# Tiles that TensorE reads, laid at different offsets modulo 512 bytes

## The chip, the core and the metric

The kernel runs on one core of a Trainium2 chip. The metric is the device time of one execution in microseconds (us); the time before is the median of 3 runs, 2656.01 us (2654.61 to 2657.22). The profile is one profiled execution of the same program. Its engines are called PE (TensorE's matmuls), PEld (TensorE's weight loads), DVE (VectorE), ACT (ScalarE), POOL (GpSimd) and SP (SyncE, which here only issues DMAs).

## The reference, cut to what matters

Two transformer blocks over 1024 tokens of width 1024, in float32:

```python
def first_block(x, p, ...):
    h = rms_norm(x, norm_mix)
    u_pool, q, k, v, g_a, g_b = jnp.split(h @ w_in, split_at, axis=-1)
    y_a = pool_mixer(u_pool, w_pool, pool_scale)
    y_b = stick_breaking_attention(q, k, v)            # 8 heads of 64
    merged = sigmoid(g_a) * (y_a @ w_branch_a) + sigmoid(g_b) * (y_b @ w_branch_b)
    x = x + merged @ w_out
    h = rms_norm(x, norm_ffn)
    x = x + (silu(h @ w_ffn_gate) * (h @ w_ffn_up)) @ w_ffn_down   # 1024 -> 2816 -> 1024
    gate = sigmoid(rms_norm(x, norm_ple) @ w_ple_gate)
    return rms_norm(x + gate * (p @ w_ple_proj), norm_final)

def second_block(x, c, ...):
    sh1, sc1, g1, sh2, sc2, g2 = split(silu(c) @ w_ada + b_ada, 6)
    h = rms_norm(x, pre_mix_g) * (1 + sc1) + sh1
    y = token_mixer(h, ...)      # chunked mLSTM beside sliding-window attention
    x = x + g1 * rms_norm(y, post_mix_g)
    h = rms_norm(x, pre_ffn_g) * (1 + sc2) + sh2
    y = conv_ffn(h, w_up, ffn_conv_w, ffn_conv_b, w_down)          # again 2816 wide
    return x + g2 * rms_norm(y, post_ffn_g)
```

## The kernel before, in words

The activations lie transposed: 128 partitions hold channels, and the free axis holds the 1024 tokens. One matmul multiplies a 128x128 block of weights (the stationary operand, loaded by its own weight load) with 512 tokens of a 128-channel tile (the moving operand) into one bank of PSUM.

Every product is made in three matmuls. A float32 operand is split into a rounded high part (type fp32r) and the rest, the low part: ACT casts `w_raw` to `w_hi` (L1853, L1618), POOL subtracts to make `w_lo` (L3991, L3897), and likewise there are `h_hi` and `h_lo` for the activations. TensorE then adds high weights by high activations, high weights by low activations, and low weights by high activations. This order stands in every loop: in `project` (L769), `halved` (L815), `qkv_steps` (L866 to L869), `beside_steps` (L1263 to L1268), `product` (L1064) and `strassen_down` (L1094). Almost all of TensorE's work has this shape.

The two feed-forward networks use a seven-product scheme. In the up and gate projections, `product(i, j)` multiplies with one of seven combinations of halves of the activations; some of these are plain halves of `h_hi` and `h_lo`, and three are kept in tiles of their own, `form_hi` and `form_lo` in block one and `back_form_hi` and `back_form_lo` in block two. In the down projection, `strassen_down` walks 77 units (7 products of 11 row tiles each). Unit u reads `x_hi` and `x_lo` of a ring of four slots (`x_hi_a`, `x_lo_a` in block one, `x_hi_b`, `x_lo_b` in block two), which ACT (L1930) and DVE (L3069) fill from `keep_x`, or from the ring `x_ring`, which SP loads from memory (L4350). These are called combination tiles and down tiles here.

Each engine runs its own list of instructions in the order of the program, and waits on semaphores that another engine or a DMA raises. No wait depends on where a tile lies.

The tiles in on-chip memory are laid out by a stack: a tile begins where the one before it on the stack ended, rounded up to 32 bytes, and a scope that is closed gives its room back, so that tiles of different stages lie over each other. The first tile, `consts`, begins at byte 16512 of each partition. `w_raw`, `w_hi` and `w_lo` are two buffers of 1024 floats each (8192 bytes a partition), and a weight block is 128 floats, which is 512 bytes a partition. A 512-token row is 2048 bytes. From `w_raw` on, the hot tiles all have sizes that are multiples of 512 bytes, so that one offset modulo 512 holds for every block and every row of a tile. The first lines of the layout are these:

```python
consts = sb("consts", [P, N_CONST])
vecs = sb("vecs", [P, N_VEC])
ident_bf = sb("ident_bf", [P, P], BF16)
causal_bf = sb("causal_bf", [P, P], BF16)
```

with `ident_bf` and `causal_bf` of 256 bytes each ahead of `mod`, `gain`, `final_gain`, `eps_col`, `w_raw`, `w_hi`, `w_lo`, `tmp`, `norm_row`, `h_hi` and `h_lo`. `consts` begins at 128 modulo 512, `ident_bf` at 288, `causal_bf` at 32, and `w_raw` at 20224, which is 256 modulo 512; so does every later tile named so far. The tiles of the second mixer (`prob`, `o_tok`, `q_carried`, `late_consts`, `rope_mem` and others) follow small tiles and begin elsewhere.

Of the kernel before, what the change touches and what calls it, by code (L numbers as in the profile page):

```python
# [9 lines left out]
BF16 = mybir.dt.bfloat16  # L10
# [4 lines left out]
P = 128  # L15
# [4 lines left out]
HALF = 512  # L20
# [190 lines left out]
KH = KD // 2  # L211
# [137 lines left out]
def two_blocks(nc, io, known=None):  # L349
    with ExitStack() as ctx:  # L350
# [9 lines left out]
        def sb_in(scope, name, shape, dt=F32):  # L360
            return scope.enter_context(nc.sbuf_tensor(name, shape, dt))

        def sb(name, shape, dt=F32):
            return sb_in(ctx, name, shape, dt)
# [1 line left out]

        consts = sb("consts", [P, N_CONST])
        vecs = sb("vecs", [P, N_VEC])
        ident_bf = sb("ident_bf", [P, P], BF16)
        causal_bf = sb("causal_bf", [P, P], BF16)  # L370
        mod = sb("mod", [P, 6 * KD])
        gain = sb("gain", [P, 4 * KD])
        final_gain = sb("final_gain", [P, 4, KD])
        eps_col = sb("eps_col", [P, 2])
        w_raw = sb("w_raw", [P, 2, 1024])
        w_hi = sb("w_hi", [P, 2, 1024], F32R)
        w_lo = sb("w_lo", [P, 2, 1024], F32R)
        tmp = sb("tmp_mem", [P, 2, T])
        norm_row = sb("norm_row", [P, T])
        h_hi = sb("h_hi", [P, KD, T], F32R)  # L380
# [46 lines left out]
        ff1 = ExitStack()  # L427
        with ExitStack() as downs:
            keep_x_a = sb_in(downs, "keep_x_a", [P, KB, HALF])
        form_hi_mem = sb_in(ff1, "form_hi", [P, 3, KH, HALF], F32R)  # L430
        with ExitStack() as downs:
            x_ring_a = sb_in(downs, "x_ring_a", [P, 4, HALF])
            x_hi_a = sb_in(downs, "x_hi_a", [P, 4, HALF], F32R)
            x_lo_a = sb_in(downs, "x_lo_a", [P, 4, HALF], F32R)
        form_lo_mem = sb_in(ff1, "form_lo", [P, 3, KH, HALF], F32R)
        with ExitStack() as forms:
            form_raw = sb_in(forms, "form_raw", [P, 8, HALF])
# [92 lines left out]
        ys = ExitStack()  # L530
# [7 lines left out]
            keep_x_b = sb_in(downs, "keep_x_b", [P, KB, HALF])  # L538
        BACK_FORMS = (SUM_2, DIFF_3, GATE_HIGH)
        with ExitStack() as raws:  # L540
            sb_in(raws, "before_back_raw", [P, 3, KH, HALF])
            back_raw = sb_in(raws, "back_raw", [P, 3, KH, HALF])
        back_hi_mem = sb_in(ys, "back_form_hi", [P, 3, KH, HALF], F32R)
        back_lo_mem = sb_in(ys, "back_form_lo", [P, 3, KH, HALF], F32R)
        x_hi_b = sb_in(ys, "x_hi_b", [P, 4, HALF], F32R)
        x_lo_b = sb_in(ys, "x_lo_b", [P, 4, HALF], F32R)
        back_sums = sb_in(ys, "back_w_sums", [P, 2, HALF])
# [4143 lines left out]
def build(nc, arrays, known=None):  # L4691
    io = {}
    for name, v in arrays.items():
        io[name] = nc.dram_tensor(f"in_{name}", v.shape, F32, kind="ExternalInput").ap()
    for name, shape in SCRATCH.items():
        io[name] = nc.dram_tensor(name, shape, F32, kind="Internal").ap()
    io["out"] = nc.dram_tensor("out_dram", (KD, P, T), F32, kind="ExternalOutput").ap()
    return two_blocks(nc, io, known)
# [12 lines left out]
```

## Time and profile before

| | |
|---|---|
| time before, median of 3 runs | 2656.01 us |
| span of the profiled execution, first to last instruction | 2657.1 us |
| PE busy | 2566.2 us, 97% of the span, 11826 matmuls |
| PEld busy | 2080.6 us, 78% |
| DVE, ACT, POOL busy | 1776.9, 1186.2, 1173.3 us |
| mean granted TensorE clock | 0.992 of full speed |
| DMA | 311.96 MB, mean 117 GB/s |

The profiled execution has no time of its own beside its span; the span lies 1.1 us above the median and inside the spread of the three runs. The busy time of a matmul in the profile is longer than the distance to the next one (a matmul of 512 columns lasts 0.39 us, and the next begins 0.23 us after it), because matmuls are pipelined and their ends are modelled. What a matmul takes of the engine is therefore read from the distance between starts. Offsets in memory do not stand in the profile; they follow from the layout.

### The profile page before, as it was taken

The page shows a single profiled execution, that of the slowest core. Times are in us where ns is not written, and L with a number is a line of the kernel's source. Part 1 is how long each engine was busy: PE and PEld are TensorE (multiplying, and loading weights), DVE is VectorE, ACT ScalarE, POOL GpSimd, SP SyncE. Part 2 cuts the span into 40 slices and gives each one's busy share as a digit, 9 for nine tenths or more (in the row PEclk, how much of TensorE's full clock was granted, in tenths as well). Part 3 has the DMA queues.
Part 4 walks back from the last instruction along what each step waited for, and adds up shares of the span by engine and source line. Part 5 has one row for each costly group of instructions (what it writes and reads, how often), then busy time and mean ns, then how long its engine had stood idle before and what let it go on. Part 6 is the DMA issues. An engine that isn't in the chain of part 4 may idle for free.

```text
span 2657.1 us, 32148 instructions
## 1 busy us (share of the span) xinstructions
PE 2566.2 (97%) x11826; PEld 2080.6 (78%) x11826; DVE 1776.9 (67%) x2180; ACT 1186.2 (45%) x2084; POOL 1173.3 (44%) x767
## 2 busy tenths in 40 slices
PE   7999999999899999999999999999999999999997
PEld 6887788888688888888877778778767888887885
DVE  6888876653877777778854546527459666666685
ACT  6777521112533333344554333455444444444444
POOL 2444522224455555555544221124442655555456
PEclk9999999999999999999999999999999999999998
DMA  3000044433155555675622111223321222225674
GB/s 125 25 25 25 20 136 158 155 122 112 48 191 197 190 199 188 219 236 184 202 79 83 65 33 40 45 58 75 135 95 48 83 84 81 86 81 182 214 234 138
DMA packets 125916, 311.96 MB, mean 117 GB/s; under 512 B 13368, under 2 KB 26936, under 8 KB 122816
## 3 DMA queue, kind: packets, MB, share of 16 engines
q1 hardware_dynamic: 125760, 309.91, 35.5%
q8 instruction: 94, 1.54, 0.3%
q14 instruction: 62, 0.51, 0.1%
HBM read 248.45 MB, written 61.41 MB: 117 GB/s over the span
## 4 chain that ended last, share of the span: by engine, by line
PE 79%; DVE 11%; ACT 3%; issue 3%; DMA 2%; POOL 2%; SPq 0%; ACTq 0%; DVEq 0%; POOLq 0%
PE psum_mem L1064 28%; PE psum_mem L769 20%; PE psum_mem L1094 11%; PE psum_mem L1263 2%; PE psum_mem L1268 2%; PE psum_mem L1265 2%; PE psum_mem L831 2%; DMA x_ring_a<-hidden 1%; PE psum_mem L815 1%; PE psum_mem L866 1%; PE psum_mem L867 1%; PE psum_mem L869 1%; PE psum_mem L1340 1%; DVE left L2769 1%; DVE tmp_mem L3696 1%
## 5 line engine op out<-in xcount | busy, mean ns | idle before, releaser
L3991 POOL TENSOR_TENSOR w_lo<-w_raw,w_hi 128x512 fp32r<-128x512 f32 x364 | 529.1, 1456 | 550.7 <-ACT w_hi L1853 531.6
L3897 POOL TENSOR_TENSOR w_lo<-w_raw,w_hi 128x1024 fp32r<-128x1024 f32 (+2 forms) x105 | 237.0, 2257 | 618.4 <-ACT w_hi L1618 531.2
L1853 ACT CAST w_hi<-w_raw 128x512 fp32r<-128x512 f32 x364 | 225.5, 620 | 387.8 <-PE psum_mem L1094 167.3
L1064 PE MATMUL psum_mem<-h_hi,w_hi 128*128 128x512 f32 x672 | 263.9, 393 | 6.6 <-ACT norm_row L2485 3.2
L1064 PE MATMUL psum_mem<-h_lo,w_hi 128*128 128x512 f32 x672 | 262.9, 391 | 1.3 <-DVE h_lo L2970 1.3
L1064 PE MATMUL psum_mem<-h_hi,w_lo 128*128 128x512 f32 x672 | 262.5, 391 | 0.0
L769 PE MATMUL psum_mem<-h_hi,w_hi 128*128 128x512 f32 x736 | 232.0, 397 | 11.6 <-ACT h_hi L1652 9.1
L769 PE MATMUL psum_mem<-h_lo,w_hi 128*128 128x512 f32 x736 | 228.5, 392 | 5.7 <-DVE h_lo L3606 5.5
L769 PE MATMUL psum_mem<-h_hi,w_lo 128*128 128x512 f32 x736 | 227.9, 391 | 2.7 <-POOL w_lo L3897 2.7
L1618 ACT CAST w_hi<-w_raw 128x1024 fp32r<-128x1024 f32 (+2 forms) x105 | 100.2, 954 | 267.9 <-PE psum_mem L769 255.3
L769 PEld LDWEIGHTS psum_mem<-h_hi,w_hi 128*128 128x128 f32 x736 | 137.9, 189 | 43.5 <-ACT h_hi L1652 9.1
L769 PEld LDWEIGHTS psum_mem<-h_lo,w_hi 128*128 128x128 f32 x736 | 138.4, 189 | 36.7 <-DVE h_lo L3606 6.9
L769 PEld LDWEIGHTS psum_mem<-h_hi,w_lo 128*128 128x128 f32 x736 | 138.6, 189 | 32.7 <-POOL w_lo L3897 3.6
L1064 PEld LDWEIGHTS psum_mem<-h_hi,w_hi 128*128 128x128 f32 x672 | 126.8, 189 | 35.3 <-ACT norm_row L2485 4.1
L1064 PEld LDWEIGHTS psum_mem<-h_lo,w_hi 128*128 128x128 f32 x672 | 127.0, 189 | 28.4 <-DVE h_lo L2970 2.4
L1064 PEld LDWEIGHTS psum_mem<-h_hi,w_lo 128*128 128x128 f32 x672 | 126.9, 189 | 26.6
L3949 POOL TENSOR_TENSOR beta<-beta,left 128x128 f32<-128x128 f32 (+2 forms) x96 | 89.4, 932 | 123.4 <-DVE left L2769 118.3
L1263 PE MATMUL psum_mem<-h_hi,w_hi 128*128 128x512 f32 x272 | 112.8, 415 | 1.1 <-DVE tmp_mem L3309 1.1
L1268 PE MATMUL psum_mem<-h_hi,w_lo 128*128 128x512 f32 x272 | 107.2, 394 | 0.0
L1265 PE MATMUL psum_mem<-h_lo,w_hi 128*128 128x512 f32 x272 | 106.6, 392 | 0.0
L1064 PE MATMUL psum_mem<-form_lo,w_hi 128*128 128x512 f32 x264 | 103.0, 390 | 1.7 <-DVE form_lo L2968 1.7
L1064 PE MATMUL psum_mem<-form_hi,w_hi 128*128 128x512 f32 x264 | 103.0, 390 | 1.4 <-ACT form_hi L1868 1.4
(465 smaller groups left out, 6330.8 us busy)
## 6 DMA issues: line engine op xcount, KB each, us to landing
hidden<-tmp_mem SPq DMA_DIRECT2D x44, 512.0 KB, 3.5
down_sums<-sum_raw SPq DMA_DIRECT2D x22, 1024.0 KB, 5.7
w_raw<-down_sums SPq DMA_DIRECT2D x88, 256.0 KB, 4.0
w_raw<-in_w_up_b SPq DMA_DIRECT2D x44, 512.0 KB, 3.7
x_ring_a<-hidden SPq DMA_DIRECT2D x66, 256.0 KB, 4.1
x_ring_b<-hidden SPq DMA_DIRECT2D x66, 256.0 KB, 4.2
w_raw<-in_w_in_a SPq DMA_DIRECT2D x32, 512.0 KB, 3.7
ada_raw<-in_w_ada SPq DMA_DIRECT2D x64, 256.0 KB, 3.3
```

Of the source, the lines that this page charges most:

```text
L769: made = e.matmul(pairs.half(use, half), wt, x[:, half_of(half)], start=at == 0 and part == 0, stop=at == len(rhs) - 1 and part == 2, skip ...
L831: return e.transpose(out, in_, ident)
L1064: made = e.matmul(out, wt, x, start=j <= DIFF_3 and k == 0 and part == 0, stop=k == KH - 1 and part == 2, skip_group_check=True)
L1094: return e.matmul(down_bank(p, mi), w_slot(w_lo if part == 2 else w_hi, slot, of)[:, block_of(mi)], (x_lo if part == 1 else x_hi)[:, u % 4 ...
L1263: e.matmul(bank(6 + half), high, h_hi[:, k, cols], start=k == 0, stop=False, skip_group_check=True)
L1265: e.matmul(bank(6 + half), high, h_lo[:, k, cols], start=False, stop=False, skip_group_check=True)
L1268: made = e.matmul(bank(6 + half), low, h_hi[:, k, cols], start=False, stop=k == KD - 1, skip_group_check=True)
L1618: e.copy(w_hi[:, i, 0:width], w_raw[:, i, 0:width]).then_inc(*S.of("w_hi", c))
L1853: e.copy(w_slot(w_hi, slot, of), source).then_inc(*S.of("w_hi", key))
L3897: e.tensor_tensor(w_lo[:, i, 0:width], w_raw[:, i, 0:width], w_hi[:, i, 0:width].bitcast(F32), ALU.subtract).then_inc(*S.of("w_lo", c))
L3949: e.tensor_tensor(kept, kept, left[i % 3][:, HALF + 1 - width:HALF + 1], ALU.mult).then_inc(*S.of("weight", i))
L3991: e.tensor_tensor(w_slot(w_lo, slot, of), source, w_slot(w_hi, slot, of).bitcast(F32), ALU.subtract).then_inc(*S.of("w_lo", key))
```

## The change

Two things are changed, both in the layout alone. The instructions, their operands' shapes, their order and their waits stay.

First, `ident_bf` moves from before `mod` to between `w_hi` and `w_lo`, and `causal_bf` from there to behind `w_lo`. Each is 256 bytes long. So `w_raw` and `w_hi` move down by 512 bytes, `w_lo` by 256, and everything from `tmp` on stays where it was.

Second, unused pads of 32 to 128 bytes go in ahead of combination tiles and down tiles. The pads push what is behind them on the same stack: in block one also `sum_raw`, `w_sums` and `parts` (by 160 bytes) and the ring `x_ring_a` (by 32), in block two also `back_raw` (by 192), `back_w_sums` and `gate_conv_in` (by 224).

| tile | offset modulo 512 before | after |
|---|---|---|
| `w_hi`, `h_hi`, `h_lo` and the other high and low activations | 256 | 256 |
| `w_lo` | 256 | 0 |
| `form_hi`, `form_lo` | 256, 256 | 288, 416 |
| `x_hi_a`, `x_lo_a` | 256, 256 | 320, 384 |
| `back_form_hi`, `back_form_lo` | 256, 256 | 352, 448 |
| `x_hi_b`, `x_lo_b` | 256, 256 | 480, 480 |

```diff
-        ident_bf = sb("ident_bf", [P, P], BF16)
-        causal_bf = sb("causal_bf", [P, P], BF16)
         mod = sb("mod", [P, 6 * KD])
...
         w_hi = sb("w_hi", [P, 2, 1024], F32R)
+        ident_bf = sb("ident_bf", [P, P], BF16)
         w_lo = sb("w_lo", [P, 2, 1024], F32R)
+        causal_bf = sb("causal_bf", [P, P], BF16)
...
+        sb_in(ff1, "before_form_hi", [P, 8])
         form_hi_mem = sb_in(ff1, "form_hi", [P, 3, KH, HALF], F32R)
         with ExitStack() as downs:
             x_ring_a = sb_in(downs, "x_ring_a", [P, 4, HALF])
+            sb_in(downs, "before_x_hi_a", [P, 8])
             x_hi_a = sb_in(downs, "x_hi_a", [P, 4, HALF], F32R)
+            sb_in(downs, "before_x_lo_a", [P, 16])
             x_lo_a = sb_in(downs, "x_lo_a", [P, 4, HALF], F32R)
+        sb_in(ff1, "before_form_lo", [P, 32])
         form_lo_mem = sb_in(ff1, "form_lo", [P, 3, KH, HALF], F32R)
...
-            sb_in(raws, "before_back_raw", [P, 3, KH, HALF])
+            sb_in(raws, "before_back_raw", [P, 3 * KH * HALF + 48])
             back_raw = sb_in(raws, "back_raw", [P, 3, KH, HALF])
+        sb_in(ys, "before_back_form_hi", [P, 24])
         back_hi_mem = sb_in(ys, "back_form_hi", [P, 3, KH, HALF], F32R)
+        sb_in(ys, "before_back_form_lo", [P, 24])
         back_lo_mem = sb_in(ys, "back_form_lo", [P, 3, KH, HALF], F32R)
+        sb_in(ys, "before_x_hi_b", [P, 8])
         x_hi_b = sb_in(ys, "x_hi_b", [P, 4, HALF], F32R)
         x_lo_b = sb_in(ys, "x_lo_b", [P, 4, HALF], F32R)
```

## Rows read from the trace of the kernel before

**Rows 1.** The page: busy time by engine, and the granted clock in 40 slices.
```profile
PE 2566.2 (97%) x11826; PEld 2080.6 (78%) x11826; DVE 1776.9 (67%) x2180; ACT 1186.2 (45%) x2084; POOL 1173.3 (44%) x767
...
PEclk9999999999999999999999999999999999999998
```

**Rows 2.** The chain of waits, merged, longest pieces: start us, us, engine, line, count.
```profile
593.98 87.22 PE psum_mem L769 x384
...
739.78 386.58 PE psum_mem L1064 x1704
...
2063.85 353.93 PE psum_mem L1064 x1560
...
2433.44 187.07 PE psum_mem L1094 x824
```

**Rows 3.** Timeline of 1000.0 to 1000.75, PE and PEld: start us, length us.
```profile
999.94 0.39 PE L1064 MATMUL psum_mem<-form_lo,w_hi 128*128 128x512 f32 x1
999.94 0.19 PEld L1064 LDWEIGHTS psum_mem<-form_hi,w_lo 128*128 128x128 f32 x1
1000.16 0.39 PE L1064 MATMUL psum_mem<-form_hi,w_lo 128*128 128x512 f32 x1
1000.17 0.19 PEld L1064 LDWEIGHTS psum_mem<-form_hi,w_hi 128*128 128x128 f32 x1
1000.39 0.39 PE L1064 MATMUL psum_mem<-form_hi,w_hi 128*128 128x512 f32 x1
```

**Rows 4.** Groups of PE matmuls, shapes apart: line, out<-in, count, busy us, mean ns.
```profile
L1064 PE MATMUL psum_mem<-h_hi,w_lo 128*128 128x512 f32 x672 | 262.5, 391 | 0.0
...
L1064 PE MATMUL psum_mem<-form_hi,w_lo 128*128 128x512 f32 x264 | 103.2, 391 | 0.8 <-POOL w_lo L3991 0.7
...
L1064 PE MATMUL psum_mem<-back_form_hi,w_lo 128*128 128x512 f32 x240 | 93.5, 390 | 0.6 <-POOL w_lo L3991 0.6
...
L1094 PE MATMUL psum_mem<-x_hi_b,w_lo 128*128 128x512 f32 x308 | 86.2, 389 | 0.0
```

**Rows 5.** Timeline of PE at four places: bf16 matmuls of 128 and of 256 columns.
```profile
1550.88 0.23 PE L1308 MATMUL psum_mem<-band_bf,ident_bf 128*128 128x128 bf16 x1
...
1550.95 0.22 PE L1308 MATMUL psum_mem<-band_bf,ident_bf 128*128 128x128 bf16 x1
...
1572.76 0.28 PE L1308 MATMUL psum_mem<-band_bf,ident_bf 128*128 128x256 bf16 x1
...
1572.88 0.27 PE L1308 MATMUL psum_mem<-band_bf,ident_bf 128*128 128x256 bf16 x1
```

**Rows 6.** Timeline of PE at three places where a float32 weight load follows.
```profile
60.51 0.39 PE L869 MATMUL psum_mem<-h_hi,w_lo 128*128 128x512 f32 x1
60.74 0.38 PE L831 MATMUL psum_mem<-consts,beta 128*128 128x128 f32 x2
...
1567.78 0.39 PE L1268 MATMUL psum_mem<-h_hi,w_lo 128*128 128x512 f32 x1
1568.01 0.38 PE L831 MATMUL psum_mem<-consts,prob 128*128 128x128 f32 x2
...
1799.59 0.39 PE L1268 MATMUL psum_mem<-h_hi,w_lo 128*128 128x512 f32 x1
1799.82 0.38 PE L1444 MATMUL psum_mem<-state,q_carried 128*128 128x129 f32 x2
```

**Rows 7.** Groups of POOL instructions on 512 elements a partition, shapes apart.
```profile
L3897 POOL TENSOR_TENSOR w_lo<-w_raw,w_hi 128x512 fp32r<-128x512 f32 x16 | 20.8, 1300 | 134.9 <-PE psum_mem L1004 82.0 <-ACT w_hi L1618 52.9
...
L4123 POOL TENSOR_TENSOR q_carried<-q_carried,qk_ml 128x512 f32<-128x512 f32 x8 | 10.1, 1267 | 5.8 <-DMA q_carried<-w_rows 5.8
```

**Rows 8.** The page's DMA issues: engine, operation, count, KB each, us to landing.
```profile
w_raw<-in_w_up_b SPq DMA_DIRECT2D x44, 512.0 KB, 3.7
x_ring_a<-hidden SPq DMA_DIRECT2D x66, 256.0 KB, 4.1
...
rope_mem<-in_rope SPq DMA_DIRECT2D x1, 1024.0 KB, 5.6
```

**Rows 9.** The chain of waits from 1125 to 1340: the first and last DMA on it.
```profile
1178.59 3.77 DMA x_ring_a<-hidden
...
1216.11 4.23 DMA x_ring_a<-hidden
```

## Prediction

> **What bounds the kernel now.** I read the page first: PE is busy 97% of the span, the next engine, DVE, 67%, and TensorE had its full clock (2.4 GHz) in all but the last slice [rows 1]. So the time can only move much if the distance between matmuls moves. The chain of waits gives that distance without the profile's rounding, as the length of an unbroken piece by its count: 87.22 / 384 = 0.2271 us in `project`, 386.58 / 1704 = 0.2269 and 353.93 / 1560 = 0.2269 in the two up projections, 187.07 / 824 = 0.2270 in the second down projection [rows 2]. One number, 0.227 us, holds in four stages, with different tiles, weight blocks and neighbours at work. The timeline shows what lies inside it: each matmul begins with the load of the next weights beside it, 0.19 us long, and the next matmul follows at 0.22 or 0.23 [rows 3].
>
> How much of 0.227 is not streaming? Two bf16 matmuls of 128 columns start 0.07 us apart, two of 256 columns 0.12 [rows 5]: 128 more columns cost 0.05 us, one column a cycle at 2.4 GHz (0.0533). So 512 columns stream in 0.2133 us, and 0.2269 - 0.2133 = 0.0136 us of each 0.227 is something else. If that is the weight load and the stream meeting in the same place of the memory, because both tiles begin at 256 modulo 512, the change removes some of it; if it is the price of changing weights, the change does nothing. This is the question to decide.
>
> **The change part by part.** It adds and removes no instruction, wait or DMA, so nothing is queued differently, and every term is a number of matmuls by a change in their distance.
>
> What meets is the stream of one matmul and the load of the next one's weights. In the order high-high, high-low, low-high the load of `w_lo` runs beside a stream of a low tile (in `project`, with two halves, also beside its own high tile), and the load of `w_hi` beside a high or low tile. Where the activations are not moved, only the loads of `w_lo` change their distance, from 0 to 256 bytes. The groups that read `w_lo` beside unmoved activations are 672 in `product` [rows 4], and 736, 272, 144, 144, 32 for `h_hi` in the other five loops and 168 for `ya_hi`, `yb_hi`, `p_hi` and `pl_hi`, counted in the code: 2168. Where the activations are moved, all three matmuls change: 3 x (264 + 240 + 2 x 308) = 3360 [rows 4], to distances from 32 to 480. Together 5528 of some 10,000 such matmuls; the other loads of `w_hi` beside `h_hi` and `h_lo` keep distance 0.
>
> The price of a changed distance is not in this trace for the pair itself, since before all of these pairs lie at distance 0. From both sides: at best the whole 0.0136 goes, 5528 x 0.0136 = 75 us; and at worst a distance that is now clean begins to collide, by at most what the rows of float32 loads allow [rows 6]: a stream of `h_hi` (at 256) with a float32 load beside it is followed at 0.23 us, which rounding lets be 0.235, 0.008 above 0.227, 5528 x 0.008 = 44 us.
>
> Between these ends I take 0. Three readings lead there. First, one view holds distance itself apart [rows 6]: after `h_hi` comes a load of `beta` (256, distance 0), of `prob` (416, distance 160) and of `q_carried` (192, distance 448), and all three follow at 0.23 us. If distance 0 cost 0.0136, the other two should stand near 0.21 or 0.22. They carry a float32 matmul behind them instead of another fp32r, but so does the first. Second, bf16 has the same extra [rows 5]: 0.07 - 0.0533 and 0.12 - 0.1067 are both about 0.01, with the load at 288 and the stream at 160 and 416 modulo 512, and with half the bytes on both sides. A collision should depend on place or on bytes; this depends on neither. Third, the load sweeps 512 bytes within 0.19 us while the stream sweeps 2048 in 0.213 [rows 3]: they run at different speeds, so a start apart by some bytes shifts a meeting and does not avoid it.
>
> The Trainium skill says the same of the ports: in "TensorE: Matmul & The Clock Gate", section "Step-by-step: what each phase is for", TensorE has two independent read ports into the on-chip memory, so that loading the next weights takes no read bandwidth from the running matmul. By that rule this change does nothing, whatever the offsets; no run here shows the ports, and the float32 loads agree as far as 0.01 us can show [rows 6].
>
> The other engines and the DMAs touch the moved tiles too. POOL makes `w_lo`, with all three operands at 256, in 1300 ns, and `q_carried`, at 192 with others, in 1267 [rows 7]: 33 ns between them, and POOL is busy 44% [rows 1], so its slack hides either. DMAs into `x_ring_a` now land at 288 modulo 512, which is 32 past a multiple of 64. A DMA to such a place stands in the trace: `rope_mem`, at 416, 1024 KB in 5.6 us, where 512 KB to a place at 256 take 3.7 [rows 8], less than double. If the landing were longer by 0.3 us (the nearest rows lie within that), it would show only where these DMAs are on the chain, 8 times from 1178.59 to 1216.11 [rows 9]: 2.4 us. I take 0.
>
> The sum is 0 against the span of 2657.1 us. The median of the runs is 1.1 us below that span, so the forecast is the median: 2656 us.
>
> **The rivals.** *Equal offsets do collide.* For it: 0.0136 us in every matmul is unexplained, and the layout has every hot tile at one offset, so no stage of the feed-forward networks can contradict it. Against it: the bf16 pairs and the float32 loads [rows 5, 6]. If all changed pairs gain, 75 us less about 2 us, because the ring's DMAs and not the matmuls are on the chain for some 40 us (40 / 0.227 x 0.0136 = 2.4) [rows 9]: 2656 - 73 = 2583 us. If only the distance of 256 frees, 2168 x 0.0136 = 29 us: 2627. The Trainium skill has a rule that points this way: in the same page, section "Back-to-back issue gap", 512 columns cost about 216 ns at full clock. By that rule 0.011 us of 0.227 could be had, an estimate of 5528 x 0.011 = 61 us; but the chain shows 0.227 at full clock [rows 2], and the page itself ties its number to matmuls measured alone.
>
> *Unequal offsets collide.* This is the slower one: distance 0 may be the clean state, in which load and stream keep out of each other's way, and any other distance costs something. Place: the same 5528 pairs, most of them in the two feed-forward networks. Price: the float32 loads read as printed [rows 6], 0.23 - 0.227 = 0.003 us, give 17 us, 2673 us; 0.008 gives 2700. It decides from 0.001 us a pair, which is 5.5 us. Against it: the `beta` row at distance 0 also stands at 0.23, so the 0.003 belongs to the float32 neighbour.
>
> That the change doesn't reach the places it names can hardly be: the offsets follow from sizes.
>
> **How the numbers follow.** No effect 0.76, with 2651 to 2661 us, the 0.2% (5.3 us) about 2656 below which a measurement of this kernel cannot tell a change from none. Equal offsets collide 0.14, in whole or in part. Unequal offsets collide, or start-of-row penalties of the same sign, 0.10. The range takes in the first case and the small prices on either side, up to 0.002 us a pair (5528 x 0.002 = 11 us): 2645 to 2668 us, and leaves out the full gain and the larger losses, some 2 in 10. So faster by over 0.2% has 0.14, within 0.2% 0.76, slower 0.10.
>
> **What would show it.** In the profile of the changed kernel the same four pieces of the chain should again come to 0.227 us a matmul. `product` is a test in itself: its matmuls with `form_hi` and `form_lo` lie at distances of 32 and 416, and those with `h_hi` and `w_hi` beside them at 0; if the first stand at 0.213 or 0.216 and the second at 0.227, equal offsets collide, and I am wrong by the first rival. If the moved ones stand above 0.228, the second rival holds. If all stand at 0.227 and the time still moves by more than 5 us, the cause is outside TensorE, and the landing of `x_ring_a` and the mean of POOL's `w_lo` are the rows to look at.

## The result: slower, and the profile after

The changed kernel takes 2675.97 us (median of four runs, 2674.84 to 2678.59) against 2656.61 for the kernel before on the same chip: a ratio of 1.0073, with a 95% interval from 1.006 to 1.0086, or about 19 us more. The profiled execution has a span of 2674.5 us, 17.4 more than before.

The page of the changed kernel, busy time by engine and the granted clock, answers to [rows 1]:

```profile
PE 2587.3 (97%) x11826; PEld 2083.7 (78%) x11826; DVE 1780.4 (67%) x2180; ACT 1187.0 (44%) x2084; POOL 1170.2 (44%) x767
...
PEclk9999999999999999999999999999999999999999
```

PE is busy 21.1 us longer with the same 11826 instructions; ACT, DVE and POOL stay within 4 us, and the granted clock stands at 9 tenths or more in every slice. So the matmuls themselves take longer. The long pieces of its chain of waits answer to [rows 2]; the change adds seven lines of code ahead of them, so L769, L1064 and L1094 are now L776, L1071 and L1101:

```profile
595.50 87.22 PE psum_mem L776 x384
...
741.18 392.44 PE psum_mem L1071 x1704
...
2072.52 344.08 PE psum_mem L1071 x1500
...
2439.92 199.67 PE psum_mem L1101 x848
```

The first piece, in `project`, is the same to the hundredth: 87.22 us for 384 matmuls, though every load of `w_lo` in it now lies 256 bytes off. The second needs 392.44 / 1704 = 0.2303 us a matmul instead of 0.2269, the third 344.08 / 1500 = 0.2294 instead of 0.2269, the fourth 199.67 / 848 = 0.2355 instead of 0.2270. The stages whose activations were moved lost; the one where only `w_lo` moved did not.

Inside a piece, the timeline of PE (start us, length us) shows which tile it is. The first product, at 1002, and the second down projection, at 2500:

```profile
1002.11 0.40 PE L1071 MATMUL psum_mem<-form_hi,w_lo 128*128 128x512 f32 x1
...
1004.21 0.40 PE L1071 MATMUL psum_mem<-form_hi,w_lo 128*128 128x512 f32 x1
...
2501.30 1.10 PE L1101 MATMUL psum_mem<-x_hi_b,w_lo 128*128 128x512 f32 x4
...
2504.10 1.10 PE L1101 MATMUL psum_mem<-x_hi_b,w_lo 128*128 128x512 f32 x4
```

Between the first two rows lie nine starts in 2.10 us, 0.233 each; between the last two twelve in 2.80, 0.233 each.

Since the two traces hold the same 11826 matmuls in the same order, each distance can be set against its own before. Where both are below 0.3 us (no wait), the matmuls on `form_hi` and `form_lo` take 5.1 us more in all, those on `back_form_hi` and `back_form_lo` 3.3, on `x_hi_a` and `x_lo_a` 3.5, on `x_hi_b` and `x_lo_b` 6.05: 18.0 us for 3323 of the 3360 moved pairs, 0.0054 us each. The other 7933 such distances gave 3.4 us more, 0.0004 each, and the longer ones, with waits in them, 3.8 us less.

About half of these 3.4 us stand right behind the moved tiles. When `product` goes from `form` or `back_form` tiles back to `h_hi` and `h_lo`, the next nine matmuls still take 28 ns more in all than before (a mean over some 60 such places), though their own distances are 0 or 256; from the tenth on nothing is left. One such place, nine and again nine starts apart:

```profile
871.21 0.39 PE L1071 MATMUL psum_mem<-h_hi,w_hi 128*128 128x512 f32 x1
...
873.29 0.39 PE L1071 MATMUL psum_mem<-h_hi,w_hi 128*128 128x512 f32 x1
...
875.33 0.39 PE L1071 MATMUL psum_mem<-h_hi,w_hi 128*128 128x512 f32 x1
```

The first nine take 2.08 us, 0.231 each, the second nine 2.04, 0.227 each. So a pair's own distance is not the whole of it: what the pairs before it did counts too, for 1.7 us in all.

### The profile page after: what moved, and what is told of

It is laid out like the page before. It is cut to its first block, busy times and chain, and to the rows that moved or that the text cites. A ratio compares the mean times of both kernels' runs of the same rounds, so it can differ in the third digit from the quotient of the medians.

```text
span 2674.5 us, 32148 instructions
## 1 busy us (share of the span) xinstructions
PE 2587.3 (97%) x11826; PEld 2083.7 (78%) x11826; DVE 1780.4 (67%) x2180; ACT 1187.0 (44%) x2084; POOL 1170.2 (44%) x767
## 4 chain that ended last, share of the span: by engine, by line
PE 79%; DVE 11%; ACT 4%; issue 3%; DMA 2%; POOL 2%; SPq 0%; ACTq 0%; DVEq 0%; POOLq 0%
PE psum_mem L1071 28%; PE psum_mem L776 20%; PE psum_mem L1101 13%; PE psum_mem L1270 2%; PE psum_mem L1275 2%; PE psum_mem L1272 2%; PE psum_mem L838 2%; PE psum_mem L822 1%; PE psum_mem L873 1%; PE psum_mem L1347 1%; DVE left L2776 1%; PE psum_mem L876 1%; PE psum_mem L874 1%; DMA x_ring_a<-hidden 1%; PE psum_mem L1312 1%
## 5 line engine op out<-in xcount | busy, mean ns | idle before, releaser
L1071 PE MATMUL psum_mem<-h_hi,w_hi 128*128 128x512 f32 x672 | 263.7, 392 | 6.3 <-ACT norm_row L2492 3.0
L1071 PE MATMUL psum_mem<-h_lo,w_hi 128*128 128x512 f32 x672 | 263.6, 392 | 1.3 <-DVE h_lo L2977 1.3
L1071 PE MATMUL psum_mem<-h_hi,w_lo 128*128 128x512 f32 x672 | 263.4, 392 | 0.0
L776 PE MATMUL psum_mem<-h_hi,w_hi 128*128 128x512 f32 x736 | 232.5, 397 | 12.6 <-ACT h_hi L1659 8.9
L776 PE MATMUL psum_mem<-h_lo,w_hi 128*128 128x512 f32 x736 | 229.0, 393 | 5.8 <-DVE h_lo L3613 5.6
L776 PE MATMUL psum_mem<-h_hi,w_lo 128*128 128x512 f32 x736 | 228.2, 391 | 2.9 <-POOL w_lo L3904 2.9
L776 PEld LDWEIGHTS psum_mem<-h_hi,w_hi 128*128 128x128 f32 x736 | 137.9, 189 | 44.6 <-ACT h_hi L1659 8.9
L776 PEld LDWEIGHTS psum_mem<-h_lo,w_hi 128*128 128x128 f32 x736 | 138.8, 189 | 36.8 <-DVE h_lo L3613 6.9
L776 PEld LDWEIGHTS psum_mem<-h_hi,w_lo 128*128 128x128 f32 x736 | 139.0, 189 | 32.9 <-POOL w_lo L3904 3.8
L1071 PEld LDWEIGHTS psum_mem<-h_hi,w_hi 128*128 128x128 f32 x672 | 126.9, 189 | 35.8 <-ACT norm_row L2492 3.9
L1071 PEld LDWEIGHTS psum_mem<-h_lo,w_hi 128*128 128x128 f32 x672 | 126.9, 189 | 30.0 <-DVE h_lo L2977 2.4
L1071 PEld LDWEIGHTS psum_mem<-h_hi,w_lo 128*128 128x128 f32 x672 | 126.9, 189 | 26.7 <-POOL w_lo L3998 0.2
L1071 PE MATMUL psum_mem<-form_lo,w_hi 128*128 128x512 f32 x264 | 104.7, 397 | 1.7 <-DVE form_lo L2975 1.7
L1071 PE MATMUL psum_mem<-form_hi,w_lo 128*128 128x512 f32 x264 | 105.4, 399 | 0.7 <-POOL w_lo L3998 0.7
```

Of the source, the lines that this page charges most:

```text
L776: made = e.matmul(pairs.half(use, half), wt, x[:, half_of(half)], start=at == 0 and part == 0, stop=at == len(rhs) - 1 and part == 2, skip ...
L1071: made = e.matmul(out, wt, x, start=j <= DIFF_3 and k == 0 and part == 0, stop=k == KH - 1 and part == 2, skip_group_check=True)
```

## The experiments

Theory D: what counts is the distance between the start of the stream and the start of the next weights, modulo something that divides 256, and at distance 0 they keep out of each other's way. The experiments can show the first part; by what means load and stream hinder each other, no run here shows. Rival O: a tile's own offset counts, 256 being a good one. Rival N: the moved tiles disturb another engine or a DMA, and matmuls only show it. Rival S: the cost comes with `w_lo`.

### Measuring the pair by itself

```
to(32 * i, f"w_{letter}"); w[i] = sb(f"w_{letter}", [P, BLOCKS * P], F32R)   # 16 weights tiles
to(32 * i, f"x_{letter}"); x[i] = sb(f"x_{letter}", [P, 512], F32R)          # 16 streams
pairs += [(0, j) for j in range(16)] + [(j, 0) for j in range(16)] + [(j, j) for j in range(16)]
```

> A kernel that only measures: one core, after one load nothing runs but fp32r matmuls of 128 x 512, 48 in each group, each with its own weight load, no wait inside a group; the reference's computation is left out. 16 groups with weights at 0 and the stream at 0, 32, ... 480 modulo 512; 16 with the stream at 0 and the weights at 0, 32, ... 480; 16 with both at the same 0, 32, ... 480. Theory D (the distance between the stream's start and the next weights' start decides): 0.227 us a matmul wherever the distance is 0 or 256, 0.229 to 0.236 at most other distances in the first two sweeps, and 0.227 in all of the third. Theory O (the stream's own offset decides, whatever the weights'): 0.229 to 0.236 off multiples of 256 in the first and third sweep, 0.227 in all of the second. Theory N (neighbours: ACT, DVE, POOL or DMAs that touch the moved tiles): 0.227 in all groups, since no neighbour runs.

The timeline of PE has one row for each group of 48 matmuls; the b-th letter stands at 32 times its place (a: 0, b: 32, c: 64, i: 256, k: 320), and (length - 0.39) / 47 is the distance in time:

```profile
62.94 11.37 PE L51 MATMUL psum_mem<-x_b,w_a 128*128 128x512 f32 x48
74.15 11.16 PE L51 MATMUL psum_mem<-x_c,w_a 128*128 128x512 f32 x48
...
141.18 11.05 PE L51 MATMUL psum_mem<-x_i,w_a 128*128 128x512 f32 x48
...
230.30 11.06 PE L51 MATMUL psum_mem<-x_a,w_a 128*128 128x512 f32 x48
241.19 11.36 PE L51 MATMUL psum_mem<-x_a,w_b 128*128 128x512 f32 x48
...
419.32 11.08 PE L51 MATMUL psum_mem<-x_b,w_b 128*128 128x512 f32 x48
```

Distance 0 gives 0.2270 and distance 256 0.2268; 64 gives 0.2291; 32 bytes either way 0.2334 and 0.2336. With both shifted alike, `x_b` with `w_b`, it is 0.2274, and all fifteen shifted pairs stand at 11.07 or 11.08. VectorE, ScalarE and GpSimd are idle from 100 to 560 us. The distance decides here; O and N can't make this.

### The two parts of the change, each alone

The first part, the low weights:

```diff
-        ident_bf = sb("ident_bf", [P, P], BF16)
-        causal_bf = sb("causal_bf", [P, P], BF16)
...
+        ident_bf = sb("ident_bf", [P, P], BF16)
         w_lo = sb("w_lo", [P, 2, 1024], F32R)
+        causal_bf = sb("causal_bf", [P, P], BF16)
```

> The first part of the change alone: ident_bf and causal_bf moved, so that the low weights begin at 0 modulo 512; no pads. Theories D, O and N: no change, within 0.2% of before (2656 +- 5 us), 0.227 us a matmul with the low weights as with the high ones, since a distance of 256 cost nothing in the changed kernel's product and project groups. The rival that the prediction priced (any unequal distance costs, 2168 pairs by 0.003 us) would have +6.5 us, 2663.

The second part, the pads:

```diff
+        sb_in(ff1, "before_form_hi", [P, 8])
         form_hi_mem = sb_in(ff1, "form_hi", [P, 3, KH, HALF], F32R)
...
+        sb_in(ys, "before_x_hi_b", [P, 8])
         x_hi_b = sb_in(ys, "x_hi_b", [P, 4, HALF], F32R)
```

> The second part alone: only the pads. Theories D, O and N all: the whole loss, 2672 to 2678 us, ratio 1.006 to 1.008, with 0.227 for streams of h_hi and h_lo and 0.229 to 0.236 for streams of the padded tiles. Here the low weights' distance to the padded tiles differs by 256 from that in the changed kernel; if the patterns by tile come out as there, distances count modulo 256.

The low weights alone took 2658.44 us against 2658.71, ratio 1.0003 (0.9994 to 1.0013). Its chain has the pieces of before again:

```profile
593.87 87.22 PE psum_mem L769 x384
739.72 386.58 PE psum_mem L1064 x1704
...
2433.36 187.07 PE psum_mem L1094 x824
```

The pads alone took 2676.38, ratio 1.0068 (1.0053 to 1.0083), and its chain has the pieces of the changed kernel:

```profile
595.16 87.22 PE psum_mem L776 x384
...
2073.58 344.13 PE psum_mem L1071 x1500
2441.09 199.67 PE psum_mem L1101 x848
```

Set against the kernel before pair by pair, the four groups of moved tiles (`form`, `back_form`, `x_a`, `x_b`) take 5.3, 3.3, 3.6 and 6.0 us more, nearly as in the changed kernel, though `w_lo` begins here at 256 and there at 0: distances count modulo 256. So the loss is the pads', as far as the two intervals can tell, and S falls: moving `w_lo` by 256 costs nothing.

### Moving the weights and leaving every stream

In the changed kernel the moved tiles are all streams. The next kernel moves the three weights tiles by 128 and no stream, by declaring the 128 bytes of `gain` behind `w_lo`:

```diff
-        gain = sb("gain", [P, 4 * KD])
...
         w_lo = sb("w_lo", [P, 2, 1024], F32R)
+        gain = sb("gain", [P, 4 * KD])
```

> No pads; the 128-byte tile gain moved from before the weights to behind them, so that w_raw, w_hi and w_lo begin at 128 modulo 512 and every stream stays at 256: a distance of 128 for nearly all of the some 10,000 fp32r pairs. Theory D: about 0.231 us a matmul everywhere (x_lo_a with the high weights, at that distance, has 0.2308 in the changed kernel), +0.004 x 9,800 = +40 us, 2690 to 2700 us. Theory O: no change, 2656 +- 5. Theory N: no change, unless POOL and ACT on the weights count, then a small one.

It took 2706.22 us, ratio 1.0174 (1.0153 to 1.0195), 47 us more; D had expected 40, priced at 0.004 us a pair, and 2700 us at most. Now `project` loses too, 89.36 / 384 = 0.2327, and `product` has 397.86 / 1704 = 0.2335:

```profile
603.18 89.36 PE psum_mem L769 x384
751.14 397.86 PE psum_mem L1064 x1704
```

The streams, still at 256, should have kept their time if their own offset counted. That 128 is a bad place for weights, whatever the streams, this kernel alone doesn't exclude. The scan does, where a stream and weights that both stand at 128 have 11.08 us, and the next kernel does for 352.

### Everything moved alike

```diff
+        sb("before_all", [P, 24])
         consts = sb("consts", [P, N_CONST])
```

> A pad of 96 bytes ahead of everything: all tiles, weights and streams alike, begin at 352 modulo 512, and every distance between hot tiles stays 0. Theory D: no change, 2658 +- 5 us, 0.227 us a matmul. Theory O (own offset): 0.231 to 0.236 as for back_form_hi at 352, +40 to +80 us. Theory N: DMAs and POOL, DVE and ACT work on every tile at 32 past a multiple of 64; if that costs, it shows here at its largest.

With every hot tile at 352 modulo 512 and every distance still 0, the kernel took 2657.9 us against 2657.78: ratio 0.9998 (0.9989 to 1.0008). `project` is at 87.22 again:

```profile
594.31 87.22 PE psum_mem L770 x384
...
2434.12 187.07 PE psum_mem L1095 x824
```

In the kernel before, neither weights nor streams stood at 352, and in the changed kernel `back_form_hi`, a stream at 352 with weights at 256 and 0, took 0.232 to 0.236. Here nothing is lost: a tile's own offset doesn't matter, nor what the move does to other engines. O and N fall in the kernel as well.

### A smaller dose

```diff
-        mod = sb("mod", [P, 6 * KD])
-        gain = sb("gain", [P, 4 * KD])
...
         w_lo = sb("w_lo", [P, 2, 1024], F32R)
+        mod = sb("mod", [P, 6 * KD])
+        gain = sb("gain", [P, 4 * KD])
```

> mod and gain, 320 bytes, moved from before the weights to behind them: w_raw, w_hi and w_lo at 448 modulo 512, all streams at 256, which is a distance of 64 modulo 256 (stream minus weights). Theory D, by the scan's 0.2291 us at that distance: +0.0023 x 9,800 = +22 us, 2675 to 2685 us, half of what weights at 128 cost. A threshold (any distance off 256 costs alike): +46 us, 2700 to 2708. Theory O: no change.

The weights stand at 448, 64 modulo 256 from the streams. It took 2675.38 us, ratio 1.007 (1.0055 to 1.0085), 18 us more; 22 were expected. In the chain `project` has 88.04 / 384 = 0.2293, against the 0.2291 of the pair measured alone:

```profile
596.91 88.04 PE psum_mem L769 x384
743.63 390.31 PE psum_mem L1064 x1704
```

The mean loss follows the distance as the scan has it; not every move away from 0 costs the same. Within `product` the three matmuls don't pay alike, though all three have the distance 64: 0.2316 us after `h_hi` with `w_hi`, 0.2261 after `h_lo`, 0.2293 after `h_hi` with `w_lo`, and 0.2290 as the mean. How they come to share it was not tried.

### Which matmuls feel it

```
groups += [[("wr_zero", name, 512)] ...]                       # fp32r
groups += [[("wb_zero", name, cols)] for cols in (512, 128) ...]   # bf16
groups += [[("wf_zero", name, 512)] ...]                       # float32
groups += [[("wr_zero", "xr_zero", 512), (name, "xf_zero", 128)] ...]   # a float32 load beside fp32r
```

> A second kernel that only measures, as the scan; the reference's computation is left out. Groups of 48 matmuls with weights at 0: fp32r streams at 0, 4, 8, 16, -16, 48, 64, 96, 128 modulo 512; fp32r streams of 384, 256 and 128 columns at 0, 64, 128; bf16 weights and streams of 512 and 128 columns at 0, 32, 64, 128; plain float32 at 0 and 128; and fp32r matmuls of 512 columns in turn with plain float32 ones of 128, whose weights lie at 0, 64 or 128. 
The bf16 groups, 512 columns, streams 0, 32, 64 and 128 bytes from the weights, then 128 columns, and the two of float32:

```profile
199.92 10.31 PE L64 MATMUL psum_mem<-xb_zero,wb_zero 128*128 128x512 bf16 x47
210.06 10.52 PE L64 MATMUL psum_mem<-xb_thirty_two,wb_zero 128*128 128x512 bf16 x47
220.42 10.52 PE L64 MATMUL psum_mem<-xb_sixty_four,wb_zero 128*128 128x512 bf16 x47
230.78 10.52 PE L64 MATMUL psum_mem<-xb_one_twenty_eight,wb_zero 128*128 128x512 bf16 x47
241.14 2.84 PE L64 MATMUL psum_mem<-xb_zero,wb_zero 128*128 128x128 bf16 x48
243.82 2.84 PE L64 MATMUL psum_mem<-xb_thirty_two,wb_zero 128*128 128x128 bf16 x48
...
251.86 41.42 PE L64 MATMUL psum_mem<-xf_zero,wf_zero 128*128 128x512 f32 x96
293.12 41.36 PE L64 MATMUL psum_mem<-xf_one_twenty_eight,wf_zero 128*128 128x512 f32 x96
```

One record is missing in each of the first four groups, so I take starts: 220.42 - 210.06 and 230.78 - 220.42 are 10.36 us for 48 matmuls, 0.2158 each, at 32 and at 64 bytes; the first, with 10.14 for 47, is at 0.2157. With 128 columns the next group starts 2.68 us later, 0.0558 each, at every distance. Float32 has 41.42 and 41.36.

A float32 matmul after an fp32r one started 316, 317 and 314.5 ns (means, the first of each series left out where it waited) behind it with its weights 0, 64 and 128 bytes off the fp32r stream. At 0.31 us an effect of a few ns could hide there. In the kernel before such pairs stand closer: after `h_hi` with `w_lo` a float32 matmul starts 231 ns later (median of 96) with `beta`, at distance 0, and 231 (median of 16) with `prob`, at 96 modulo 256.

None of these feels the distance; D had expected up to half the effect for bf16 and 0.004 to 0.007 us for the float32 load. Theory R, 0.0136 us over streaming in every group, fails too: bf16 is 0.0025 over it. Of the kinds tried, only fp32r weights loaded beside an fp32r stream feel the distance; fp32r weights beside a bf16 or float32 stream were not tried at other distances.

It shrinks with fewer columns too. The groups at distances 0, 64 and 128, with 384 and 256 columns:

```profile
141.48 8.48 PE L64 MATMUL psum_mem<-xr_zero,wr_zero 128*128 128x384 f32 x48
149.81 8.48 PE L64 MATMUL psum_mem<-xr_sixty_four,wr_zero 128*128 128x384 f32 x48
158.12 8.60 PE L64 MATMUL psum_mem<-xr_one_twenty_eight,wr_zero 128*128 128x384 f32 x48
166.56 5.91 PE L64 MATMUL psum_mem<-xr_zero,wr_zero 128*128 128x256 f32 x48
172.31 5.82 PE L64 MATMUL psum_mem<-xr_sixty_four,wr_zero 128*128 128x256 f32 x48
```

At 384 columns 128 bytes cost 0.12 / 47 = 0.0026 us and 64 nothing, where D had expected the same as at 512; at 256 columns distance 0 is the slower one. So the size of the loss does not follow D's picture of collisions in time.

### Is any distance better than 0?

```
x[i] = sb(name, [P, 512 + i % 8], F32R)[:, i % 8:]   # 64 streams, 4 bytes apart; weights at 0
```

> A third kernel that only measures, as the scan; the reference's computation is left out. Weights at 0, fp32r streams of 512 columns at 0, 4, 8, ... 252 bytes, 64 groups of 48 matmuls. The question is whether any distance is better than 0, where 0.2268 us is still 0.011 above the 0.2158 of bf16. Theory D, if 0 is the best case of the same collisions: nothing below 0.2265, all other distances 0.228 to 0.238, 64 the lowest of the multiples of 32. If the 0.011 is collisions too and some distance avoids them: some group at 0.216 to 0.224, most likely within 16 bytes of 0 or of 64, and the kernel laid out at that distance would gain 0.003 to 0.011 x 9,800 = 29 to 108 us.

Streams at 20, 28, 32, 64, 96, 128, 160, 192 and 224 bytes:

```profile
118.14 11.68 PE L47 MATMUL psum_mem<-x_af,w_mem 128*128 128x512 f32 x48
...
140.87 11.05 PE L47 MATMUL psum_mem<-x_ah,w_mem 128*128 128x512 f32 x48
151.75 11.36 PE L47 MATMUL psum_mem<-x_ba,w_mem 128*128 128x512 f32 x48
...
240.92 11.15 PE L47 MATMUL psum_mem<-x_ca,w_mem 128*128 128x512 f32 x48
...
330.15 11.36 PE L47 MATMUL psum_mem<-x_da,w_mem 128*128 128x512 f32 x48
...
419.61 11.36 PE L47 MATMUL psum_mem<-x_ea,w_mem 128*128 128x512 f32 x48
...
509.17 11.41 PE L47 MATMUL psum_mem<-x_fa,w_mem 128*128 128x512 f32 x48
...
598.89 11.37 PE L47 MATMUL psum_mem<-x_ga,w_mem 128*128 128x512 f32 x48
...
688.89 11.36 PE L47 MATMUL psum_mem<-x_ha,w_mem 128*128 128x512 f32 x48
```

The longest of all 64 are 11.68 us (0.2402, at 20, 132, 196 and 244 bytes), the shortest 11.04 and 11.05 (0.2266 and 0.2268, at 28, 60 and 156 bytes among others). D had expected every distance but 0 between 0.228 and 0.238; it missed at both ends. None is below the 11.05 of distance 0 by more than a row's rounding. So the scan offers no layout of these tiles that beats the kernel before.

## Why the prediction was wrong

**The bound was read rightly.** PE sets the time, and the time moved nearly as far as the distances between matmuls moved: 21.3 us more in the short ones, 3.8 less in those with waits, 17.4 in the span.

**The terms outside TensorE were right at 0.** POOL's `w_lo` on 512 elements takes 1301 ns after 1300 [rows 7], and the ring's DMAs, now 32 bytes off a multiple of 64, land in 3.9 us after 4.1 [rows 8].

**The step that failed is "Between these ends I take 0".** The price of a changed distance in the moved tiles is 0.0054 us on average, inside the 0.008 that I had as the upper end; that end was no bound, since it was read from float32 loads, and 20 bytes cost 0.0134. The fine scan gives nearly the whole sum without the kernel. Against the 11.05 of distance 0, distances of 32, 96, 192 and 224 cost 0.31 or 0.32 / 47 = 0.0066 to 0.0068 us, 128 the same, 160 0.0077 and 64 0.0021. `form_hi` at 32 (two of three) and `form_lo` at 160 make 264 x 0.0209 = 5.5 us; `back_form_hi` at 96 and `back_form_lo` at 192 make 240 x 0.0200 = 4.8; `x_hi_a` at 64 and `x_lo_a` at 128 make 308 x 0.0108 = 3.3; `x_hi_b` and `x_lo_b` at 224 make 924 x 0.0066 = 6.1. The sum is 19.7 us; the trace has 18.0, and the runs about 19. The one group that is well off is `back_form`, 4.8 against 3.3: after `back_form_lo` the next start comes at 0.2262 us, as before, where the scan of one pair has 0.2336. In `x_a` the sum fits while single pairs do not: 0.2321 after `x_hi_a` with `w_lo`, where the scan has 0.2291, and 0.2310 after `x_lo_a`, where it has 0.2334. In the kernel pairs of different distances alternate, and the nine slow matmuls behind the moved tiles show that one pair acts on the next ones; by what rule stays open.

**The three readings that led to 0 did not bear on the question.** The first compared float32 loads at distances 0, 160 and 448 [rows 6]: a float32 load did not feel the distance at any place tried, so these rows would have looked alike under either rival. The second took the same extra of 0.01 in bf16 [rows 5] as proof that bytes and place don't count. Measured over 48 matmuls, each with its load, the extra of bf16 is 0.0558 - 0.0533 = 0.0025 us, against 0.2268 - 0.2133 = 0.0135 for fp32r at distance 0: a price of changing weights that both share is refuted. The pairs that I read do stand further apart: all 32 of them in the trace of the kernel before are 66 or 67 ns apart at 128 columns and 119 or 120 at 256, an extra of about 0.013. Each is a single pair behind matmuls of another kind, not a run of its own kind; why that costs more was not tried. So the extra was read rightly, and it was likened to fp32r's by a number alone. The third, that a shift only moves a meeting since load and stream run at different speeds, is refuted by the scan: 4 bytes can change a matmul by 0.01 us.

The Trainium skill's rule is that TensorE's two read ports keep the load from the running matmul ("TensorE: Matmul & The Clock Gate", "Step-by-step: what each phase is for"). The bf16 groups agree with it, 0.2158 at every distance. For 512 columns at full clock the Trainium skill gives about 216 ns, as the gap of a matmul measured alone (the same page, "Back-to-back issue gap"). The bf16 groups show that number in a run of 48, each with its load. For fp32r both differ from the measurement, 0.2268 at best and 0.2334 at most multiples of 32, and the measurement decides.

**The count was half right.** Of the 5528 pairs, the 2168 with only `w_lo` moved cost nothing: 256 is as good as 0, and for that the forecast of 0 held, though not for its reason. The slower rival, "Unequal offsets collide", had the dependence on distance, the sign and 2673 us, at a chance of 0.10. That its 5528 x 0.003 = 17 us is near the 3360 x 0.0054 = 18 is luck: one factor was too large, and the other came from float32 rows, which do not feel the distance. What stood against it, the `beta` row, was right that the 0.003 belongs to the float32 neighbour, and said nothing about fp32r pairs. The faster rival falls with the fine scan: no distance is better than 0. In no run here did a distance remove the 0.011 us by which fp32r at its best exceeds bf16, and its cause stays open.

**The test that I named worked.** `product` told it as written: matmuls on `form_hi` and `form_lo` stand above 0.228, at 0.2313 to 0.2348, and those on `h_hi` with `w_hi` at 0.227 on average.

## What to carry to other kernels

Where fp32r tiles of 512 columns stream over fp32r weights, lay the two a multiple of 256 bytes apart: a small tile or a pad declared between them cost this kernel, which TensorE bounds, 0.7% to 1.7% with no instruction changed. With 256 columns no such loss was seen at the two distances tried. Before a row is taken as a control for a cost, ask whether it has the same data type and could show the cost at all. And a row rounded to 0.01 us cannot exclude 0.005 us, which over the 5528 pairs is 28 us, more than the range that was given.

## What the runs showed of the hardware

The cost of a distance changes from one step of 4 bytes to the next, the finest tried, and has no simple order: 20 bytes cost 0.0134 us a matmul, 28 nothing, 32 0.0066.

The fourth piece of the changed kernel's chain holds a second, smaller loss. It begins after PE has stood for 2.76 us, waiting for `x_lo_b`:

```profile
2439.92 1.57 PE L1101 MATMUL psum_mem<-x_lo_b,w_hi 128*128 128x512 f32 x4 [2.76 <-DVE x_lo_b L3076]
```

Windows of the changed kernel (us, PE busy, ..., PEclk the last but two) show the clock at its lower level, 1.2 GHz, for part of the next four microseconds:

```profile
2417.00:2440.00 23.00, 20.24 (x88) 15.86 (x86) 12.08 (x12) 10.57 (x17) 9.25 (x7) 1.00 0.68 229
2440.00:2444.00 4.00, 4.00 (x11) 3.17 (x12) 3.90 (x4) 2.06 (x5) 2.87 (x3) 0.57 0.00 0
2444.00:2448.00 4.00, 4.00 (x19) 3.23 (x18) 3.14 (x4) 0.43 (x1) 1.39 (x1) 1.00 0.64 209
```

Seven matmuls there start 0.427 us apart, about 1.4 us lost. The kernel before waits for `x_lo_b` in the same stage too, 2.90 us, and has full clock behind it (granted clock 1.00 from 2417 to 2437); the kernel with the pads alone shows the fall again. Why the clock falls in the one and not in the other was not tried.
